# Turning x's quads at other places, storing the rotation and the first tables later, and a second buffer for the S5 outputs in a two-layer trunk on one core

## What is computed

```
for i in range(2):
    h = rms_norm(x, norm_mix[i])
    x = x + (gmlp(h) if i == 0 else s5(h))
    x = x + (silu(h2 @ w1[i]) * (h2 @ w3[i])) @ w2[i]        # h2 = rms_norm(x, norm_ffn[i])
    x = x + sigmoid(rms_norm(x, norm_ple[i]) @ w_gate[i]) * (p[i] @ w_proj[i])
return rms_norm(x, norm_final)

s5: u = h @ w_in; per group of 16 channels a diagonal complex state of 64 is driven by u,
    scanned over the 256 tokens, read out, y + d * u; g = gelu(y); val, gate = split(g @ w_out)
    return val * sigmoid(gate)
```

## Time and profile before

| | |
|---|---|
| median of 3 runs | 2235.43 us (2235.05 to 2237.21) |
| profiled execution, its own time | 2235.3 us |
| its span | 2233.3 us (2.0 us lie around it) |
| PE busy | 2217.8 us, 99% |
| VectorE, ScalarE, GpSimd busy | 1448.8, 1024.9, 493.1 us |
| DMA | 531 MB, mean 238 GB/s |
| clock granted to PE | 1.00 over the run, lower only in the last slice |

### The profile page before, as it was taken

The page is one execution under the profiler, slowest core; times in us unless marked ns, Lnnn a source line. Parts: engine busy times, 40 slices in busy tenths (PEclk is TensorE's granted clock), DMA queues, the critical chain, the costliest instruction groups (busy, mean ns, idle before and its releaser), DMA issues.

```text
span 2233.3 us, 28436 instructions
## 1 busy us (share of the span) xinstructions
PE 2217.8 (99%) x11280; PEld 1833.5 (82%) x11280; DVE 1448.8 (65%) x1612; ACT 1024.9 (46%) x1234; POOL 493.1 (22%) x470
## 2 busy tenths in 40 slices
PE   9999999999999999999999999999999999999998
PEld 7888888888888888888887788888888888888887
DVE  7879776667676666666668876555554445555666
ACT  5544444444434444445444454544444344444454
POOL 1246145456665544301003100000000000000001
PEclk9999999999999999999999999999999999999999
DMA  8668898988887898888789877777776667777774
GB/s 304 186 204 232 265 279 250 258 248 238 262 244 225 243 279 247 265 245 269 231 258 352 305 233 210 217 223 221 210 217 207 196 190 225 219 215 229 233 230 147
DMA packets 350677, 531.04 MB, mean 238 GB/s; under 512 B 106209, under 2 KB 127089, under 8 KB 349905
## 3 DMA queue, kind: packets, MB, share of 16 engines
q1 hardware_dynamic: 339456, 491.64, 73.5%
q0 software_dynamic: 8320, 30.75, 3.9%
q10 hardware_dynamic: 2768, 6.83, 0.9%
HBM read 475.67 MB, written 53.48 MB: 237 GB/s over the span
## 4 chain that ended last, share of the span: by engine, by line
PE 96%; DMA 1%; DVE 1%; issue 0%; ACT 0%; SPq 0%; ACTq 0%; DVEq 0%
PE PS L1636 62%; PE PS L1642 31%; DMA RAW<-in_s_w_out 1%; DMA X<-in_x 0%; DMA HT<-zd 0%; PE PS L1903 0%; PE PS L1904 0%; PE PS L1902 0%; PE PS L1740 0%; PE PS L1729 0%; DVE OP L1136 0%; PE PS L1667 0%; PE PS L1825 0%; DVE WLO L1110 0%; PE PS L1850 0%
## 5 line engine op out<-in xcount | busy, mean ns | idle before, releaser
L1636 PE MATMUL PS<-WHI,OP 128*128 128x512 f32 x6208 | 1537.8, 390 | 1.8 <-ACT YP L1023 1.4
L1110 DVE TENSOR_TENSOR WLO<-RAW,WHI 128x1024 fp32r<-128x1024 f32 x783 | 1020.5, 1317 | 687.8 <-ACT WHI L821 683.5
L1636 PEld LDWEIGHTS PS<-WHI,OP 128*128 128x128 f32 x6208 | 1162.3, 188 | 246.2 <-issue 3.6
L821 ACT ACTIVATE WHI<-RAW 128x1024 fp32r<-128x1024 f32 x783 | 827.5, 1062 | 999.6 <-PE PS L1642 644.7
L1642 PE MATMUL PS<-WLO,OP 128*128 128x512 f32 x3104 | 829.7, 389 | 1.3 <-DVE WLO L1110 1.3
L1642 PEld LDWEIGHTS PS<-WLO,OP 128*128 128x128 f32 x3104 | 582.5, 188 | 122.7 <-DVE WLO L1110 1.7
L805 POOL TENSOR_TENSOR ON<-X,GF 128x1024 f32<-128x1024 f32 x3 | 9.9, 3316 | 941.0 <-DVE X L1463 941.0
L706 POOL TENSOR_TENSOR TA<-BRAW,FAC 128x64 f32<-128x64 f32 x16 | 10.7, 669 | 267.4 <-DMA BRAW<-in_s_b_im 267.4
L869 ACT ACTIVATE S<-PS,RC 128x512 f32<-128x512 f32 x66 | 41.7, 684 | 37.0 <-PE PS L1642 36.9
L1136 DVE SCALAR_TENSOR_TENSOR OP<-HT,VEC,OP 128x128 fp32r<-128x128 f32 x120 | 38.2, 392 | 12.9 <-ACT OP L845 12.8
L1122 DVE TENSOR_TENSOR OP<-HT,OP 128x512 fp32r<-128x512 f32 x50 | 35.9, 760 | 15.4 <-ACT OP L836 15.4
(11 more groups left out here) (215 smaller groups left out, 956.6 us busy)
## 6 DMA issues: line engine op xcount, KB each, us to landing
RAW<-in_ffn_w SPq DMA_DIRECT2D x528, 512.0 KB, 4.3
RAW<-in_gm_w_in SPq DMA_DIRECT2D x64, 512.0 KB, 4.3
RAW<-in_s_w_out SPq DMA_DIRECT2D x64, 512.0 KB, 4.6
RAW<-in_ple_w_gate SPq DMA_DIRECT2D x56, 512.0 KB, 4.5
zd<-ZT SPq DMA_DIRECT2D x40, 512.0 KB, 3.2
HT<-zd SPq DMA_DIRECT2D x160, 128.0 KB, 5.0
RAW<-in_gm_w_out SPq DMA_DIRECT2D x32, 512.0 KB, 5.5
RAW<-in_s_w_in SPq DMA_DIRECT2D x32, 512.0 KB, 5.7
```

What stands on the lines that cost most here:

```text
L821: A_.activation(hi_of(t), raw_of(t), ACT.Copy).then_inc(hi_ready, 1)
L1110: V_.tensor_tensor(lo_of(t), raw_of(t), hi_of(t).bitcast(F32), ALU.subtract).then_inc(lo_ready, 1)
L1636: T_.matmul(dst[:, th, :], x_part, hi_of(t)[:, f], start=first and kk == 0 and part == 0, stop=False)
```

## The change

There are four edits.

1. `turn(1)` moves into tile 0, between its 8 matmuls with the high part and its 4 with the low part (`between`); `turn(2)` stays behind tile 1, and `turn(3)` moves behind tile 2.
2. The four rotation stores on SP move from behind loads U+8, U+10, U+12, U+14 to behind loads U+20, U+24, U+28, U+32. The loop over blocks stays behind them in the text.
3. POOL's wait ahead of the clearing of `EXP[1]` goes from `split_used` at U+6 to U+12.
4. `YP` gets a second buffer in the place of `Z`, used by duos 5 and 7. `take_y` waits for the last earlier duo of the same buffer, and, for the second one, until `Z` has been read for the last time as input of `UT`. `y_high(4)` moves one tile on, and where both fall on one tile `take_y` now comes first.

```diff
+Y_HOME = [0, 0, 0, 0, 0, 1, 0, 1]
+HIGH_AT = [t + (d == DUOS - 4) for d, t in enumerate(Y_AT)]
...
-        YP = place("YP", [P, 2, T, 2, CH], at=s_at)
+        YP = [place(f"YP{i}", [P, 2, T, 2, CH], at=(s_at, z_at)[i]) for i in range(2)]
...
             for i in range(4):
-                loads_to(start("up0a") + 8 + 2 * i)
+                loads_to(start("up0a") + 20 + 4 * i)
...
-                    pool.wait_ge(split_used, start("up0a") + 6)
+                    pool.wait_ge(split_used, start("up0a") + 12)
...
             def take_y(d):
                 act.wait_ge(out_of, d + 1)
-                if d:
-                    act.wait_ge(yg_ready, d)
+                if Y_HOME[d]:
+                    act.wait_ge(ut_ready, NT)
+                earlier = [e for e in range(d) if Y_HOME[e] == Y_HOME[d]]
+                if earlier:
+                    act.wait_ge(yg_ready, earlier[-1] + 1)
...
                 for d in range(DUOS):
-                    if W0 + g == Y_AT[d]:
-                        y_high(d)
                     if W0 + g == OUT_AT[d] + 1:
                         take_y(d)
+                for d in range(DUOS):
+                    if W0 + g == HIGH_AT[d]:
+                        y_high(d)
...
-            def tile(t, dst, block_, first, last_one):
+            def tile(t, dst, block_, first, last_one, between=None):
...
+                if between is not None:
+                    turn(between)
                 pe.wait_ge(lo_ready, t + 1)
...
-                        tile(t, acc(stage, n), block_ + TK * k, j == 0, j == depth - 1)
+                        tile(t, acc(stage, n), block_ + TK * k, j == 0, j == depth - 1, between=1 if t == 0 else None)
...
             turn(0)
-            turn(1)
 
             def prologue(t):
-                if t == 1:
-                    turn(2)
-                    turn(3)
+                if t in (1, 2):
+                    turn(t + 1)
```

More of the change, by code:

```diff
@@ L1019, in take_y @@
                 act.wait_ge(out_of, d + 1)
-                if d:
-                    act.wait_ge(yg_ready, d)
+                if Y_HOME[d]:
[3 more added lines that the diff above has]
+                    act.wait_ge(yg_ready, earlier[-1] + 1)
                 for g in range(2):
-                    last = A_.activation(YP[:, :, :, g, :].rearrange("p b i c -> p b c i"),
+                    last = A_.activation(YP[Y_HOME[d]][:, :, :, g, :].rearrange("p b i c -> p b c i"),
                                          PS[:, OUT_BANK[d] + g, 0:2 * P].rearrange("p (b c i) -> p b c i", b=2, i=T),
@@ L1547, in turn_y @@
                 V_.transpose(YG[:, :, :, :].rearrange("p b i k -> p (b i k)"),
-                             YP[:, :, :, :, :].rearrange("p b i g c -> p (b i g c)")).then_inc(yg_ready, 1)
+                             YP[Y_HOME[d]][:, :, :, :, :].rearrange("p b i g c -> p (b i g c)")).then_inc(yg_ready, 1)
             def y_low(d):
```

## The result

The changed kernel takes 2252.7 us, the median of 6 runs (2251.74 to 2255.43), against 2235.39 us of the kernel before, 6 runs beside it (2234.96 to 2237.21). The ratio is 1.0078, with a 95% interval of 1.0065 to 1.0091. It is 17.3 us slower; forecast were 17.6.

What follows compares the result with a forecast made beforehand. PE, busy for 99% of the span, was taken to set the time. From 2235.3 us, -0.1 - 1.3 - 1.4 + 18.9 + 1.5 = +17.6 gave 2252.9 us; range for 8 in 10: 2248.5 to 2260.

Steps and rivals of the forecast that it cites:

- Edit 2, what is queued behind: SP issues block 1's BRAW 47 us later, behind the moved rotation stores; PE then waits 18.9 us at taps (15.8 to 29.6).
- arrival: From the end of tile U+25 to POOL's start on block 1: 7.1 us, bounds 4.9 and 10.5.
- POOL's block 1: POOL's work on block 1 before the first taps: 20.0 us, bounds 19.1 and 27.3, with DVE mostly idle.
- restart: After the long wait at taps PE resumes at a slow clock: +1.5 us, bounds 0 and 3.
- low-part wait: PE's 1.27 us wait at 316.71 goes as stores and POOL's work move away, either likely enough: -1.3 us.
- edit 1: At the start PE still idles until 8.3 us, but the wait before x's fourth quad goes: -0.1 us (+0.3 to -1.3).
- edit 4: take_y(5) need not wait for YG, so PE's 1.37 us wait at 1247.88 goes: -1.4 us, other bound 0.
- the 0.9 us added for caution: POOL's time for block 1 before taps was taken as 20.0 us, near the low bound of 19.1.
- The small credit for the fourth quad: PE's 0.20 us wait at 15.68 for x's fourth quad goes, saving slightly more than itself.
- the late parameters are free: Rival: slack at the first taps absorbs block 1's late parameters, only gains remain, 2232.5 us; 4%.
- the crowded queue: Rival: crowded queue and slow POOL for block 1, a wait of 25 to 29.6 us, 2259 to 2264 us; 10%.
- the second wait: Rival: SP, waiting for block 1, issues no weight loads; 3 to 5 us more behind taps, 2256 to 2258 us; 8%.

Runs made afterwards that it cites:

- mended version: Changed kernel with block 1's parameters at the old place, turn(1) ahead of tile 0 again, take_y(5) one tile earlier: 2233.08 us, ratio 0.999; again 2234.35 us, 0.9991.
- PE kept busy: Changed kernel plus 150 useless transposes of the unit matrix on PE ahead of the first pair's wait for DT: 2252.57 us, ratio 1.0078.

## Why the forecast was right

**What bounds the kernel.** Right: PE's busy time stayed, its idle time moved.

**Edit 2, what is queued behind.** Right in mechanism and nearly in size. The experiments show it from both sides: edit 2 alone gives 1.0087, and the whole change with only the two loads put back gives 0.9995. The terms, forecast and measured in after (the rows of edits 1 and 4 are differences of two profiled executions):

| | forecast | measured |
|---|---|---|
| arrival, from the end of tile U+25 to POOL's start | 7.1 | 6.3 |
| POOL's block 1 | 20.0 | 19.06 |
| `taps` due after the same point | 8.25 | 8.3 |
| wait | 18.9 | 17.1 |
| restart | 1.5 | 1.35 |
| low-part wait (edits 2 and 3) | -1.3 | -1.3 (no entry left) |
| edit 1 | -0.1 | +0.2 (fifth tile starts at 22.28, before 22.06) |
| edit 4 | -1.4 | -0.6 (wait 0.77 for 1.37) |
| sum | 17.6 | 16.75; the span grew by 16.4 |

The two halves of the wait were each taken about 0.9 us too large, the gains 1.1 us too large; these errors cancel in part. The profiled run is also the shortest of its six: its own time is 16.4 us above the profiled one of before, the medians are 17.3 apart. The rows of edits 1 and 4 lie within the scatter: the fifth tile starts at 21.8 to 23.3 us in four profiles with the old order and at 21.95 to 23.7 in five others with the new one, and PE's wait for `YP` goes from none to 1.4 us without edit 4. So the agreement of the medians within 0.2 us is luck in part; the sum's terms were good to about 1 us each.

**The size of POOL's block** was the term with the widest bounds, 19.1 to 27.3, and 19.06 lies at the low one by luck. DVE was not mostly idle. It idled until 369.57, then had three low parts to make, the ones behind block 1's `QT` that the prediction itself names as in store after `taps`. The timeline of DVE in after:

```profile
369.57 1.25 DVE L1488 STREAM_TRANSPOSE QS<-QT 128x1024 f32<-128x1024 f32 x1 [15.23 <-POOL QT L727]
370.74 5.80 DVE L1116 TENSOR_TENSOR WLO<-RAW,WHI 128x1024 fp32r<-128x1024 f32 x3
```

And of POOL, the same operation beside these low parts and after them:

```profile
371.22 2.04 POOL L743 TENSOR_TENSOR TB<-CT,LAMA 128x512 f32<-128x512 f32 x1
...
377.44 1.06 POOL L746 TENSOR_TENSOR TB<-CT,LAMA 128x512 f32<-128x512 f32 x1
```

Three operations (L743 to L745) took 2.04, 2.12 and 1.93 us, their counterparts without one beside them (L746, L747, L742) 1.06, 1.26 and 1.07. That is 2.7 us; without the low parts the block would have taken about 16.4 us, an estimate from these rows. The forecast's parts came out as 1.8 for the small operations (2.5 forecast), 7.0 for `QT` (8.0), 0.6 for `BB` (0.6) and 9.65 for `DT` (8.0). The 8.0 was itself no pace of POOL alone: block 0's `DT` had run beside the eight L1136. So two parts too large and one too small made 19.1, and the 0.9 us added for caution was not needed.

The prediction gave 18.0 us for the wait by the rule of the Trainium skill ("SBUF — State Buffer", section "Who interferes with whom"), which has a DVE instruction with two inputs in SBUF and a GpSimd one that reads SBUF lock each other out. It took DVE as idle, and DVE was not. The trace agrees with the rule, by the 2.04 against 1.06 us above, but not with that use of it, and that 17.1 is near 18.0 is no support. With more low parts beside it the block took 20.9 us (the stores four loads earlier) and 27.3.

**The restart** was right, 1.35 us for 1.5: forecast from 12 transposes at the start of the run, it was measured behind a stall in the middle.

**Edit 4 was mis-sized**: the step that failed is "Even if it began only there, its 1.1 us would be over at 1245.9". It left out that in the new order, which the rows of the order showed, two high parts stand between `take_y(4)` and `take_y(5)`, and the second waits for its load. That "PE has no wait for one in this stage in the list" was true and no help: the wait for that load was covered by the one for `YG`, and came up when this went (3.97 us in after, 3.76 with edit 4 alone; with edit 1 alone, where ACT waited 1.91 us for `YG` instead of 3.64, it waited 0.68 us more for that load). The entry for `YP`, which the prediction expected to be gone, stayed at 0.8 us; how much the edit took off it is open, as the table of profiles shows. A list of PE's waits shows only the last of the conditions; the next one must be looked up on ACT, the engine ahead of PE.

**Edit 1** behaved as described (1.18 us for the operands in place of 1.25 for x), down to PE's start at 8.56 against 8.3 forecast. The small credit for the fourth quad can't be seen: the fifth tile starts 0.2 us later, within the scatter of the start.

**Edits 2 and 3** remove the low-part wait, and either does so alone, as forecast. The reason was named too evenly: without the store the eight operations still take 6.19 us instead of 7.55, without POOL 2.19, store or not.

**The rivals.** That the late parameters are free fell with a wait of 17.1 us; the crowded queue with an arrival of 6.3 and a block of 19.06; the second wait did not occur, as PE's list has no further entry of more than 0.8 us beyond the start. DVE's first low part after the stall could have made one: DVE idled 8.4 us ahead of it for ACT's high part, which stood behind 16 small copies. The low parts in store covered it.

## What to carry to other kernels

- In a queue written out by hand, a wait that is moved moves everything written behind it. Before a store is put off, read down its issuer's list to the first thing that someone waits for, and compare that delay with the slack at the consumer: here 47 us of delay against 18.7 of slack, for two loads of 32 KB each.
- When a wait is taken away, look on the engine that caused it, not on the one that waited, for the idle time that ends next. `take_y(5)` came free of one wait and stood behind another that had always been there.
- When PE is busy for 99%, the listed waits are the ceiling of what removing them can win: 4.2 us here. The mended version has got about 2 of them, at the edge of what can be told. Waits of about 1 us also come and go between profiles where no edit touches them, so a single profile doesn't price such an edit.

## What was not expected of the hardware

- The restart does not cost more behind a longer stall. After PE had stood for 8.9, 17.1 and 18.8 us, `taps` took 1.93, 1.93 and 1.94 us instead of 1.08, and the following high part 3.30, 2.61 and 3.11 instead of 2.14 (both as with PE kept busy): in all 2.0, 1.3 and 1.8 us, in one profile each. This could not be foreseen from the start of the run.
- The first high part of the run takes about 2.1 us in eight profiled executions and 3.0 to 3.6 in four (3.44 with edit 1 alone, 2.10 in after, though both have the same order there). The fifth tile starts between 21.4 and 22.3 us behind a short one and between 23.3 and 23.7 behind a long one. One of the profiles with a long one (the stores four loads earlier) shows a granted clock of 0.50 there, the others show 1.00 over it. This is some 1.5 us of scatter that no edit made, as large as the gains that were looked for; its cause is open.
- Eight operations of 128x128 on DVE with two inputs in SBUF take 2.19 us beside an idle POOL and 6.19 to 7.59 beside a busy one, a factor of about 3. The other way round, POOL's operations of 128x512 take 1.06 to 1.26 us in after with no low part on DVE beside them and 1.93 to 2.12 beside one.
